# A fused kernel's third block: attention in six batches, with the input blocks reordered between them

## The chip, the cores and the metric

One Trainium2 chip, one core. The metric is the device time of the whole program in microseconds (us), the median of three runs. The program is one launch that computes three transformer blocks one after the other on 256 tokens of width 1024.

## What is computed

The first two blocks (a pooling mixer with a SwiGLU, and latent attention with a SwiGLU) and what follows the third block's mixer (cross-attention to a memory of 256 tokens, an FFN with a convolution, the last norm) are not touched. The third block's mixer is, cut to what matters:

```python
z = rms_norm(x, mix_norm_g) @ w_in                      # 256 x 1024 by 1024 x 2328
q, kc, vc, ks, vs, kw, vw, gl, zg, zc = split(z)        # 512, 6 x 128, 24, 512, 512

# attention: 8 heads of 64, two groups of 4 heads share keys and values
k_cmp, v_cmp = compress(kc), compress(vc)               # 15 blocks of 32 tokens, gelu MLP
o_c = softmax(mask(q @ k_cmp)) @ v_cmp
o_s = softmax(causal(q @ ks)) @ vs                      # all 4 blocks of 64 are selected
o_w = softmax(causal(q @ kw)) @ vw                      # the window is longer than the sequence
y_nsa = g[..., 0] * o_c + g[..., 1] * o_s + g[..., 2] * o_w     # g = sigmoid(gl)

# gMLP: u, v = gelu(zg); per chunk of 128 tokens and group: a causal 128 x 128 matrix
y_gmlp = u * (w_s @ layer_norm(v) + b_s)

# convolution: a, gt = zc; 31 taps along the tokens, each of 256 channels by itself
y_conv = silu(layer_norm(conv31(a * sigmoid(gt))))

y = concat(rms_norm(y_nsa), rms_norm(y_gmlp), rms_norm(y_conv))
x = x + y @ w_out
```

Everything is float32.

## The kernel before, in words

**Engines and order.** Each engine has its own program, written out by hand: SP issues the weight loads, ACT, DVE, POOL (GpSimd) and PE follow, and semaphores tie them. An engine runs its instructions in the written order, so what waits holds up all that is written behind it.

**Weights** come as blocks of 1 MB (`raw`, three buffers). ACT rounds a block to its upper part `wh` (L555), DVE subtracts to get the lower part `wl` (L968). A call `after(name)` in ACT's or DVE's program makes the part of the block three places behind `name`. PE multiplies a block as three products, upper by upper, upper by lower, lower by upper (`three`, L1629 to L1631): 48 matmuls of 256 columns for a block, 24 for the narrow z_gl. Blocks of the mixer are z_a and z_gt (the convolution's two inputs), z_v and z_u (the gMLP's), z_kcvc (to be compressed), z_q0 and z_q1 (queries), z_ksw and z_vsw (keys and values of both branches), z_gl (gates); then mem6 and mem7, the last two blocks of the memory's values, and four of `w_out`.

**The convolution** is shared. `hc` = a * sigmoid(gt) (two channel halves, c = 0 and 1) is made by DVE at L1264 from z_gt's tanh on ACT (L785). DVE does all 31 taps of c = 0. POOL does the taps 0 to 24 of c = 1, a multiplication (L1581) and an addition (L1584) for each, and DVE the last six of c = 1 (L1282). DVE's list is `VECTOR_TAPS`: 25 taps of c = 0, then in turn (25,0), (25,1), (26,0), ... Tap (25,1) waits for POOL's last one. Fourteen of DVE's 37 taps are written ahead of the attention loop, then four in each unit, so (25,1) comes in unit 3.

**The attention** is a loop of 16 units, one for each head and branch. In a unit DVE adds the mask to the scores in the bank and takes the row maxima in one custom instruction (L1383), negates (L1386); ACT exponentiates (L849) and sums; DVE makes the reciprocal times the gate (L1392, L1393); ACT scales the probabilities by it (L863); PE transposes them (3 of 128x128, L2087); ACT copies them to SBUF (L857); PE multiplies by the values (3 products, L2099 to L2101) into the two banks in which the compressed branch already lies. Scores run two units ahead (L2048). Between transposes and P.V stand nine matmuls of mem6 or mem7, or four dummy matmuls of 512 columns (`turn_over`, L2120), 24 in all.

**The rest of the mixer.** The compressed branch: four transfers of kc and vc on ACT's queue, 64 small matmul records (L2004), scores (L2026), softmax on DVE (L1360 ff.), eight transfers on ACT's queue that place v_cmp as a block diagonal `vbd` (L830), and the product with it (L2079). The gMLP: gelu of z_v and z_u (DVE L1290 to L1295), the mix (L2064, L2068). The output product reads `yn`, turned on PE (L1646) and split in upper and lower parts (ACT L575, DVE L977).

The list, and how a tap waits:

```python
VECTOR_TAPS = ([(k, 0) for k in range(POOL_TAPS)]
               + [(k, c) for k in range(POOL_TAPS, TAPS) for c in range(2)])
                        if (k - 1, c) in VECTOR_TAPS:
                            dve.wait_ge(cv_tap, VECTOR_TAPS.index((k - 1, c)) + 1)
                        else:
                            dve.wait_ge(cv_tap_pool, k)
```

Of the kernel before, what the change touches and what calls it, by code (L numbers as in the profile page):

```python
# [75 lines left out]
TAPS_BEFORE = 14  # L76
TAPS_PER_STEP = 4
# [4 lines left out]
U_MEM = {6: 3, 7: 9}  # L82
MEM_PER_STEP = 3
MEM_STEPS = -(-NT * KD // MEM_PER_STEP)

U_TURN, U_STATS, U_LN, U_SILU, U_SQUARES, U_TURN_Y, U_SPLIT = 7, 8, 9, 10, 11, 13, 14
# [56 lines left out]
def weight_blocks(w):  # L143
# [59 lines left out]
    cols("z_v", win, zg + GW, GW)  # L203
    cols("z_u", win, zg, GW)
    cols("z_kcvc", win, z, 2 * P)
# [4 lines left out]
    cols("z_gl", win, z + 6 * P, 24)  # L210
    mem(6)
# [11 lines left out]
def build(nc, w, consts, bands, out):  # L223
# [17 lines left out]
    with ExitStack() as ctx:  # L241
# [17 lines left out]
        ksw = sb("ksw", [P, GROUPS, 2, SEQ])  # L259
        con = sb("con", [P, NCONST])  # L260
# [12 lines left out]
        REGION = 61312  # L273
# [4 lines left out]
        def at_(name, shape, dt=F32, off=None):  # L278
# [4 lines left out]
            for d in shape[1:]:  # L283
# [56 lines left out]
        kcm = at_("kcm", [P, NCMP])  # L340
# [6 lines left out]
        p2_0 = at_("p2_0", [P, 3 * P])  # L347
# [7 lines left out]
        s2 = [kvc[:, :, :].rearrange("p a s -> p (a s)")[:, 0:3 * P],  # L355
              fl[:, :, :, :, :].rearrange("p a k g n -> p (a k g n)")[:, GG * P:GG * P + 3 * P]]
        p2 = [p2_0, at_("p2_1", [P, 3 * P])]
        nst = at_("nst", [P, 4, 2 * NSA_HEADS, NT])
        lst = at_("lst", [P, 64])

        uu, vg = yn[:, :, 3 * GW:4 * GW], yn[:, :, 0:GW]
        ws = fl[:, :, :, :, :].rearrange("p a k g n -> p (a k g n)")[:, 0:GG * P]
# [171 lines left out]
        def _(act):  # L534
# [248 lines left out]

            act.wait_ge(block_used, at["z_gt"] + 1)
            act.activation(e1[:, :], bank[1][:, :], ACT.Tanh, scale=0.5).then_inc(z_out, 1)  # L785
            hi(at["z_a"] + 3)
            after("z_gt")
            for i, name in enumerate(("z_v", "z_u")):
                act.wait_ge(block_used, at[name] + 1)
                b = bank[2 + i]  # L790

                act.wait_ge(*((hc_done, 1) if i == 0 else (gz_d, 3)))
                act.activation(e1[:, :], b[:, :], ACT.Square).then_inc(gz_a, 1)
                act.wait_ge(gz_d, 3 * i + 2)
                act.activation(e1[:, :], e2[:, :], ACT.Tanh, scale=GELU_S).then_inc(gz_a, 1)
                after(name)
            act.wait_ge(block_used, at["z_kcvc"] + 1)
            act.activation(kvc[:, :, :].rearrange("p a s -> p (a s)"), bank[0][:, :], ACT.Copy).then_inc(z_out, 1)
            act.wait_ge(z_out, 2)
            for g in range(GROUPS):  # L800

                act.dma_start(x4[0:DH, :, g, :], kvc[g * DH:(g + 1) * DH, :, :]).then_inc(shifted, 16)
                act.dma_start(x4[DH:P, :, g, 0:SEQ - 1], kvc[g * DH:(g + 1) * DH, :, 1:SEQ]).then_inc(shifted, 16)
            after("z_kcvc")
            for i in range(2):
                act.wait_ge(block_used, at[f"z_q{i}"] + 1)
                act.activation(qt[:, 2 * i:2 * i + 2, :].rearrange("p a s -> p (a s)"), bank[1 + i][:, :],
                               ACT.Copy).then_inc(z_out, 1)
                after(f"z_q{i}")

            act.wait_ge(cmp_mm, 1)
            hs = bank[7][0:DH, 0:60]
# [3 lines left out]
            act.wait_ge(block_used, at["z_ksw"] + 1)  # L816
            act.wait_ge(ksw_zero, 1)
            for g in range(GROUPS):
                rows_ = slice(g * DH, (g + 1) * DH)
                ins = act.activation(ksw[rows_, g, :, :].rearrange("p a s -> p (a s)"), bank[3][rows_, :], ACT.Copy)  # L820
            ins.then_inc(z_out, 1)
            after("z_ksw")
            act.wait_ge(cmp_mm, 2)
# [129 lines left out]
        def _(dve):  # L953
# [1302 lines left out]
```

## Time and profile before

| | |
|---|---|
| median of 3 runs | 968.39 us (966.55, 968.39, 970.23) |
| the profiled execution | 968.99 us, of which the profile's span is 967.0 us |
| mean granted clock of PE over the span | 0.989 |
| PE busy in the span | 917.7 us |
| the mixer's stretch on PE | 540.16 (first matmul of z_a) to 699.37 us |

Times in the rows are us from the span's start. A row's duration of a matmul is longer than the distance to the next one's start, since matmuls overlap, so distances between starts are what they cost. "x3" is a count of records; a float32 product outside `three` is recorded as more than one.

### The profile page before, as it was taken

The page shows a single profiled execution, that of the slowest core. Times are in us where ns is not written, and L with a number is a line of the kernel's source. Part 1 is how long each engine was busy: PE and PEld are TensorE (multiplying, and loading weights), DVE is VectorE, ACT ScalarE, POOL GpSimd, SP SyncE. Part 2 cuts the span into 40 slices and gives each one's busy share as a digit, 9 for nine tenths or more (in the row PEclk, how much of TensorE's full clock was granted, in tenths as well). Part 3 has the DMA queues.
Part 4 walks back from the last instruction along what each step waited for, and adds up shares of the span by engine and source line. Part 5 has one row for each costly group of instructions (what it writes and reads, how often), then busy time and mean ns, then how long its engine had stood idle before and what let it go on. Part 6 is the DMA issues. An engine that isn't in the chain of part 4 may idle for free. (4 is left out here: it accounts for less than half of the span.)

```text
span 967.0 us, 16772 instructions
## 1 busy us (share of the span) xinstructions
PE 917.7 (95%) x6406; PEld 852.4 (88%) x6406; DVE 536.5 (55%) x882; ACT 476.7 (49%) x768; POOL 339.5 (35%) x189
## 2 busy tenths in 40 slices
PE   4999999999999999999999999897999989999996
PEld 4999999999987899999999999686798789999995
DVE  3884443345556574444435495775465576666655
ACT  5754444334555574334444442586454465555542
POOL 2264333440000064444333279701100154444441
PEclk9999999999999999999999999798999999999999
DMA  9677665642431767666644665201343577666601
GB/s 305 201 230 227 195 193 179 182 130 81 148 131 45 226 202 233 179 184 195 194 154 131 176 157 187 88 1 44 131 174 87 153 215 214 179 178 192 195 23 43
DMA packets 187405, 154.33 MB, mean 160 GB/s; under 512 B 6573, under 2 KB 172685, under 8 KB 187357
## 3 DMA queue, kind: packets, MB, share of 16 engines
q1 hardware_dynamic: 184941, 148.67, 50.6%
q0 software_dynamic: 752, 2.39, 1.0%
q10 hardware_dynamic: 1664, 2.60, 0.8%
q8 instruction: 33, 0.54, 0.3%
q14 instruction: 15, 0.12, 0.0%
HBM read 152.04 MB, written 1.05 MB: 158 GB/s over the span
## 5 line engine op out<-in xcount | busy, mean ns | idle before, releaser
L1538 POOL TENSOR_TENSOR dl<-draw,dh 128x1024 fp32r<-128x1024 f32 x66 | 241.4, 3659 | 287.0 <-ACT dh L599 286.9
L1629 PE MATMUL bank<-xh,wh 128*128 128x256 f32 x1192 | 338.1, 284 | 1.4 <-DVE xl L1189 0.7
L1631 PE MATMUL bank<-xh,wl 128*128 128x256 f32 x1192 | 337.1, 283 | 0.0
L1630 PE MATMUL bank<-xl,wh 128*128 128x256 f32 x1192 | 337.0, 283 | 0.0
L1629 PEld LDWEIGHTS bank<-xh,wh 128*128 128x128 f32 x1192 | 227.4, 191 | 4.8 <-DVE wl L968 1.3
L1630 PEld LDWEIGHTS bank<-xl,wh 128*128 128x128 f32 x1192 | 227.6, 191 | 2.2
L1631 PEld LDWEIGHTS bank<-xh,wl 128*128 128x128 f32 x1192 | 227.6, 191 | 0.1
L968 DVE TENSOR_TENSOR wl<-raw,wh 128x2048 fp32r<-128x2048 f32 (+5 forms) x53 | 112.4, 2127 | 60.4 <-ACT wh L555 60.4
L1068 DVE TENSOR_TENSOR wl<-raw,wh 128x2048 fp32r<-128x2048 f32 x57 | 137.5, 2412 | 1.4 <-ACT wh L622 1.4
L622 ACT ACTIVATE wh<-raw 128x2048 fp32r<-128x2048 f32 x57 | 108.8, 1909 | 8.5 <-DMA raw<-in_ffn_w_up 8.5
L1629 PE MATMUL bank<-dh,hh 128*128 128x512 f32 x264 | 103.4, 392 | 3.7 <-DVE hl L1074 3.7
L1631 PE MATMUL bank<-dh,hl 128*128 128x512 f32 x264 | 103.4, 392 | 0.0
L1630 PE MATMUL bank<-dl,hh 128*128 128x512 f32 x264 | 103.3, 391 | 0.0
L555 ACT ACTIVATE wh<-raw 128x2048 fp32r<-128x2048 f32 (+5 forms) x53 | 93.6, 1772 | 19.2 <-PE bank L1631 8.3
L608 ACT ACTIVATE th<-bank 128x256 f32<-128x256 f32 x44 | 16.8, 382 | 173.9 <-PE bank L1631 171.7
L1518 POOL TENSOR_SCALAR st<-ss 128x1 f32<-128x1 f32 x18 | 10.8, 602 | 236.2 <-ACT junk L564 236.1
L1058 DVE SCALAR_TENSOR_TENSOR ga<-th,bank 128x256 f32<-128x256 f32 x44 | 18.5, 420 | 134.9 <-ACT th L608 134.9
L599 ACT ACTIVATE dh<-draw 128x1024 fp32r<-128x1024 f32 x66 | 69.6, 1055 | 10.7 <-PE bank L1631 10.7
L1074 DVE TENSOR_TENSOR hl<-pr,hh 128x256 fp32r<-128x256 f32 x66 | 29.8, 452 | 63.5 <-ACT hh L636 63.5
L1629 PEld LDWEIGHTS bank<-dh,hh 128*128 128x128 f32 x264 | 49.8, 189 | 12.9 <-issue 4.0
L1629 PE MATMUL bank<-wh,xh 128*128 128x512 f32 (+3 forms) x182 | 60.0, 330 | 0.0
L1631 PEld LDWEIGHTS bank<-dh,hl 128*128 128x128 f32 x264 | 49.6, 188 | 10.8
(301 smaller groups left out, 1440.3 us busy)
## 6 DMA issues: line engine op xcount, KB each, us to landing
raw<-in_ffn_w_up SPq DMA_DIRECT2D x88, 512.0 KB, 6.1
draw<-in_ffn_w_down SPq DMA_DIRECT2D x66, 512.0 KB, 3.5
raw<-in_ffn_w_gate SPq DMA_DIRECT2D x44, 512.0 KB, 5.3
raw<-in_w_in SPq DMA_DIRECT2D x18, 512.0 KB, 5.0
raw<-in_xattn_wk SPq DMA_DIRECT2D x8, 512.0 KB, 4.7
raw<-in_mla_w_o SPq DMA_DIRECT2D x8, 512.0 KB, 3.9
raw<-in_xattn_wv SPq DMA_DIRECT2D x8, 512.0 KB, 4.5
raw<-in_w_out SPq DMA_DIRECT2D x8, 512.0 KB, 4.4
```

Source lines behind the costliest of these rows:

```text
L555: ins = act.activation(h, r, ACT.Copy)
L599: act.activation(dh[s][:, :], draw[s][:, :], ACT.Copy).then_inc(d_hi, 1)
L608: act.activation(th[s][:, :], b[:, 0:SEQ], ACT.Tanh, scale=0.5).then_inc(tanh_done, 1)
L622: act.activation(wh[ns][:, :], raw[ns][:, :], ACT.Copy).then_inc(hi_done, 1)
L968: ins = dve.tensor_tensor(l, r, h.bitcast(F32), ALU.subtract)
L1058: dve.scalar_tensor_tensor(out=ga[:, :], in0=th[s][:, :], scalar=1.0, in1=g, op0=ALU.add, op1=ALU.mult).then_inc(gated, 1)
L1068: dve.tensor_tensor(wl[ns][:, :], raw[ns][:, :], wh[ns][:, :].bitcast(F32), ALU.subtract).then_inc(lo_done, 1)
L1074: dve.tensor_tensor(hl[s][:, :], pr[s][:, :], hh[s][:, :].bitcast(F32), ALU.subtract) \
L1538: pool.tensor_tensor(dl[s][:, :], draw[s][:, :], dh[s][:, :].bitcast(F32), ALU.subtract) \
L1629: pe.matmul(outp, a_hi, b_hi, start=start, stop=False, **kw)
L1630: pe.matmul(outp, a_hi, b_lo, start=False, stop=False, **kw)
L1631: return pe.matmul(outp, a_lo, b_hi, start=False, stop=stop, **kw)
```

## The change

The mixer is written in another order, and its attention in another form.

- The blocks' order becomes z_a, z_gt, z_q0, z_q1, z_ksw, z_vsw, z_gl, z_kcvc, z_v, z_u, mem6, mem7. z_vsw, z_v, z_u, mem6 and mem7 are multiplied in two halves, with pieces of attention between them.
- The attention goes in six batches (`BATCHES`: token tile t, branch, first head, heads in each group). A batch has two banks, one for each group, each with 512 columns of scores: four heads by 128 keys (t = 0) or two by 256 (t = 1). PE starts a bank with identity times mask (`identr`, `maskr`) and adds the scores. DVE takes the maxima with one reduction for a bank, ACT exponentiates straight from the bank, PE turns four tiles, ACT copies 512 columns, PE multiplies by the values. Reciprocal and gate are applied behind P.V (`acc_evict`), the compressed branch is added by DVE (`comp_add`).
- The dummy matmuls, the scaling of the probabilities and the custom maxima are gone.
- DVE's taps are placed by `conv(first, last)` between the blocks' parts. POOL does its 25 taps in one piece; the load and cut of w_s stand ahead of them, the load of the last norm's gain behind the attention.
- The eight `vbd` transfers stand on ACT behind the exponentials of batch 3.

The diff, cut (a line of "..." marks what is left out):

```diff
+BATCHES = ((0, 0, 0, 4), (0, 1, 0, 4), (1, 0, 0, 2), (1, 0, 2, 2), (1, 1, 0, 2), (1, 1, 2, 2))
+HEADS_DONE = [sum(GROUPS * x[3] for x in BATCHES[:b]) for b in range(len(BATCHES) + 1)]
...
@@ ACT's program @@
+            def nsa_exp(b, g):
+                t, br, j0, n = BATCHES[b]
...
+                for j in range(n):
+                    h = g * REP + j0 + j
+                    act.activation(s2[g][:, j * keys:(j + 1) * keys], bank[g][:, j * keys:(j + 1) * keys], ACT.Exp,
+                                   scale=NSA_SCALE, bias=nst[:, 1, t, br, h:h + 1],
+                                   accum_out=nst[:, 2, t, br, h:h + 1]).then_inc(n_exp, 1)
...
+            nsa_pt(2, 1)
+            gelu_tanh(1)
+            nsa_exp(3, 1)
+            after("z_u")
             act.wait_ge(cmp_mm, 2)
...
             for h in range(NSA_HEADS):
                 act.dma_start(vbd[h * NCMP:(h + 1) * NCMP, h * DH:(h + 1) * DH], vcs[:, h // REP, :]) \
                    .then_inc(vbd_set, 16)
...
+            nsa_pt(3, 0)
+            nsa_exp(4, 0)
...
@@ DVE's program @@
+            def acc_evict(t, br):
+
+                dve.wait_ge(o_all, (2, 4, 8, 12)[2 * t + br])
+                r = nst[:, 3, t, br, :]
+                then(dve.reciprocal(r, nst[:, 2, t, br, :]))
+                then(dve.tensor_tensor(r, r, gv[:, t, 1 + br, :], ALU.mult))
...
+                if br == 1:
+                    dve.wait_ge(acc_out, 2 * t + 2)
+                    return dve.tensor_tensor(yn[:, t, 0:HALF], yn[:, t, 0:HALF], acc2[:, :], ALU.add)
...
+            conv(24, 26)
+            after("z_gl")
+            nsa_max(1)
...
             after("z_kcvc")
+            conv(26, 29)
+
+            gelu_in(0)
+            nsa_max(2)
+            gelu_out(0)
...
+            after("mem7")
+            dve.wait_ge(comp_in, NT)
+            acc_evict(1, 1).then_inc(y_nsa, 1)
+            split_t(6, xh, xl, C_MOUT, 0, range(4, KD))
...
@@ POOL's program @@
             pool.wait_ge(hc_done, 1)
-            conv(0, 2)
+            conv(0, POOL_TAPS)
             layer_norm_rstd(0, 12, 20)
-            conv(2, 11)
...
@@ PE's program @@
+            def nsa_scores(b):
+                t, br, j0, n = BATCHES[b]
+                keys = (t + 1) * P
+                pe.wait_ge(n_exp, HEADS_DONE[b])
+                for g in range(GROUPS):
+
+                    o = bank[g][:, :].rearrange("p (j s) -> p j s", j=n)[:, :, t * P:keys]
+                    pe.matmul(o, identr[:, :], maskr[:, :].rearrange("p (a s) -> p a s", a=1).to_broadcast([P, n, P]),
+                              start=True, stop=False, skip_group_check=True)
+                    for j in range(n):
+                        ins = pe.matmul(bank[g][:, j * keys:(j + 1) * keys], qt[:, j0 + j, t * P:(t + 1) * P],
+                                        ksw[:, g, br, 0:keys], start=False, stop=True, skip_group_check=True)
+                ins.then_inc(n_mm, 1)
...
+            nsa_turn(1, 1)
+            nsa_pv(1, 0)
+            pe.wait_ge(gz_d, 3)
+            tokens_half("z_u", 3, 0, xh, xl)
+            nsa_pv(1, 1)
+
+            nsa_scores(3)
+            nsa_turn(2, 0)
+            tokens_half("z_u", 3, 1, xh, xl)
...
+            pe.wait_ge(y_scaled, 4)
+            turn(yn, 0, range(4, KD))
```

How the instructions stand now, at three places. DVE, from the weight pass behind z_kcvc to gelu_out of z_v (`yc` is the convolution's sum, `e_...` are the gelu's scratch tiles, `x_111` holds the gMLP's u and v, `nst` the maxima):

```order
L988 TENSOR_TENSOR wl<-raw,wh 128x2048 [waits hi_done,fl_done]
L1302 SCALAR_TENSOR_TENSOR yc<-hc,col,yc 128x256 [waits cv_tap_pool]
L1302 SCALAR_TENSOR_TENSOR yc<-hc,col,yc 128x256 [waits cv_tap] x2
L1319 TENSOR_SCALAR e_127<-e_125 128x512 [waits gz_a]
L1321 TENSOR_TENSOR e_126<-e_127,bank 128x512 [waits gz_d]
L1311 TENSOR_REDUCE nst<-bank 128x2 [waits n_mm]
L1311 TENSOR_REDUCE nst<-bank 128x2
L1315 TENSOR_SCALAR nst<-nst 128x2x2 [waits dve_order]
L1325 SCALAR_TENSOR_TENSOR x_111<-e_125,bank 128x512 [waits gz_a]
```

Before, the tap that waits for POOL stood in the attention loop, in unit 3, between the maxima of one unit and the reciprocals (DVE, before):

```order
L1386 TENSOR_SCALAR nst<-nst 128x2 [waits dve_order]
L1282 SCALAR_TENSOR_TENSOR yc<-hc,col,yc 128x256 [waits cv_tap_pool]
L1282 SCALAR_TENSOR_TENSOR yc<-hc,col,yc 128x256 [waits cv_tap] x3
L1392 RECIPROCAL nst<-nst 128x2 [waits n_exp]
L1393 TENSOR_TENSOR nst<-nst,gate 128x2 [waits dve_order]
```

The tap moved to a place ahead of gelu_in, of the maxima of batch 2 and of gelu_out. PE, from the scores of batch 2 to z_u's first half (`s_0`, `s_1` are the exponentials of the two groups, `gain` the room of the copied probabilities, `con` the identity):

```order
L2046 MATMUL bank<-maskr,identr 128x2x128 [waits n_exp]
L2049 MATMUL bank<-ksw,qt 128x256 x2
L2046 MATMUL bank<-maskr,identr 128x2x128
L2049 MATMUL bank<-ksw,qt 128x256 x2
L2059 MATMUL bank<-con,s_0 128x128 [waits n_out,n_exp]
L2059 MATMUL bank<-con,s_0 128x128 x3
L2123 MATMUL bank<-fl,cw_113 64x30 [waits z_ws,fl_done]
L2123 MATMUL bank<-fl,cw_113 64x30 x31
L2059 MATMUL bank<-con,s_1 128x128 [waits n_out,n_exp]
L2059 MATMUL bank<-con,s_1 128x128 x3
L2072 MATMUL bank<-vsw,gain 128x64 [waits n_out]
L2072 MATMUL bank<-vsw,gain 128x64 x3
L1662 MATMUL bank<-wh,xh 128x256 [waits lo_done,gz_d]
```

The semaphore `gz_d` is counted by the gelu's steps on DVE; z_u's first matmul waits for L1325 above. ACT, around the `vbd` transfers, before:

```order
L824 ACTIVATE kcm<-bank 128x15 [waits cmp_mm]
L825 ACTIVATE vcs<-bank 15x128
L830 DMA vbd<-vcs 15x64 [waits vbd_zero,cmp_out]
L830 DMA vbd<-vcs 15x64 x7
L833 ACTIVATE vsw<-bank 128x512 [waits block_used]
```

and now:

```order
L879 ACTIVATE vcs<-bank 15x128
L883 DMA vbd<-vcs 15x64 [waits cmp_out]
L883 DMA vbd<-vcs 15x64 x7
L820 ACTIVATE gain<-bank 128x512 [waits o_all,n_t]
L812 ACTIVATE s_0,nst<-bank,nst 128x256 [waits n_t,n_max]
L812 ACTIVATE s_0,nst<-bank,nst 128x256
```

What stands behind the transfers is now the copy of batch 3's probabilities and batch 4's exponentials; before, it was the copy of z_vsw.

## Rows read from the trace of the kernel before

**Rows 1.** page, part 1: busy time, share of the span, instructions
```profile
PE 917.7 (95%) x6406; PEld 852.4 (88%) x6406; DVE 536.5 (55%) x882; ACT 476.7 (49%) x768; POOL 339.5 (35%) x189
```

**Rows 2.** windows: stretch, length, busy us (records) of each engine, clock, DMA, GB/s
```profile
540.16:604.00 63.84, 62.93 (x563) 61.75 (x562) 40.91 (x52) 23.24 (x28) 39.71 (x36) 1.00 0.64 183
...
608.80:619.00 10.20, 9.49 (x25) 5.44 (x24) 6.09 (x20) 2.72 (x11) 9.39 (x10) 0.51 0.56 205
619.00:663.40 44.40, 37.95 (x279) 35.18 (x280) 31.05 (x126) 32.14 (x100) 7.22 (x11) 1.00 0.07 25
663.40:666.80 3.40, 3.40 (x17) 3.22 (x17) 2.06 (x11) 2.12 (x8) 0.39 (x1) 0.54 0.02 5
...
677.00:699.37 22.37, 21.10 (x98) 17.19 (x96) 11.06 (x14) 10.01 (x14) 2.17 (x5) 1.00 0.43 142
```

**Rows 3.** waits of PE, 540 to 702: total us, times, longest
```profile
PE bank L2099 <- ACT p L857: 7.6, 5, 2.6
```

**Rows 4.** timeline of PE: start, us, line, operation, count
```profile
563.20 0.28 PE L1629 MATMUL bank<-xh,wh 128*128 128x256 f32 x1
...
580.57 3.92 PE L2004 MATMUL bank<-fl,cw 128*64 128x30 f32 x64
...
632.56 0.50 PE L2087 MATMUL bank<-con,kvc 128*128 128x128 f32 x3
632.90 0.82 PE L2048 MATMUL bank<-ksw,qt 128*128 128x128 f32 x4
633.37 0.47 PE L1629 MATMUL bank<-wh,mh 128*128 128x256 f32 x1
...
635.23 0.50 PE L2087 MATMUL bank<-con,fl 128*128 128x128 f32 x3
...
682.03 0.40 PE L1631 MATMUL bank<-wh,xl 128*128 128x512 f32 x1
682.26 0.40 PE L1629 MATMUL bank<-wh,xh 128*128 128x512 f32 x1
```

**Rows 5.** groups of PE by form, 540 to 700: busy, mean ns, idle before
```profile
L2004 PE MATMUL bank<-fl,cw 128*64 128x30 f32 x64 | 3.9, 221 | 0.0
L2079 PE MATMUL bank<-vbd,e 120*128 120x512 f32 x4 | 3.8, 1101 | 0.5 <-ACT e L844 0.5
L2026 PE MATMUL bank<-kcm,qt 64*128 64x15 f32 x32 | 3.3, 259 | 0.0
```

**Rows 6.** timeline of ACT: z_gt's tanh, and the vbd transfers' issue
```profile
551.88 0.60 ACT L785 ACTIVATE e<-bank 128x512 f32<-128x512 f32 x1 [9.12 <-PE bank L1631]
...
593.98 8.88 ACTq L830 DMA_DIRECT2D vbd<-vcs  x8
```

**Rows 7.** timeline of DVE: product hc, a weight pass, taps
```profile
558.72 0.68 DVE L1264 SCALAR_TENSOR_TENSOR hc<-e,bank 128x512 f32<-128x512 f32 x1
...
605.34 2.41 DVE L968 TENSOR_TENSOR wl<-raw,wh 128x2048 fp32r<-128x2048 f32 x1 [3.66 <-ACT wh L555]
...
621.36 2.65 DVE L1282 SCALAR_TENSOR_TENSOR yc<-hc,col,yc 128x256 f32<-128x256 f32 x4
...
631.83 1.67 DVE L1282 SCALAR_TENSOR_TENSOR yc<-hc,col,yc 128x256 f32<-128x256 f32 x4
```

**Rows 8.** groups of POOL by form, 553 to 626
```profile
L1581 POOL TENSOR_SCALAR tapped<-hc,col 128x256 f32<-128x256 f32 x24 | 33.0, 1376 | 2.1
L1584 POOL TENSOR_TENSOR yc<-yc,tapped 128x256 f32<-128x256 f32 x24 | 21.5, 894 | 2.0
```

**Rows 9.** timeline of POOL in its taps
```profile
605.70 3.10 POOL L1581 TENSOR_SCALAR tapped<-hc,col 128x256 f32<-128x256 f32 x1
...
615.74 0.92 POOL L1581 TENSOR_SCALAR tapped<-hc,col 128x256 f32<-128x256 f32 x1
...
617.57 0.92 POOL L1581 TENSOR_SCALAR tapped<-hc,col 128x256 f32<-128x256 f32 x1
...
622.26 0.86 POOL L1584 TENSOR_TENSOR yc<-yc,tapped 128x256 f32<-128x256 f32 x1
```

More of the change, by code:

```diff
@@ new lines, in _ @@
+            nsa_exp(1, 0)
+            after("z_kcvc")
+            nsa_pt(0, 1)
+            nsa_exp(1, 1)
+            gelu_square(0)
+            nsa_pt(1, 0)
+            gelu_tanh(0)
+            nsa_exp(2, 0)
+            after("z_v")
+            nsa_pt(1, 1)
+            nsa_exp(2, 1)
+            act.wait_ge(cmp_mm, 1)
+            hs = bank[2][0:DH, 0:60]
+            act.activation(hg[:, 0, :], hs, ACT.Square).then_inc(cmp_a, 1)
+            act.wait_ge(cmp_d, 2)
+            act.activation(hg[:, 1, :], hg[:, 2, :], ACT.Tanh, scale=GELU_S).then_inc(cmp_a, 1)
@@ L895, in _ @@
-            act.wait_ge(o_all, 2 * NSA_HEADS)
+            nsa_pt(3, 1)
+            nsa_exp(4, 1)
+            nsa_pt(4, 0)
+            mem_block(6)
+            after("mem6")
+            nsa_exp(5, 0)
+            nsa_pt(4, 1)
+            nsa_exp(5, 1)
+            act.wait_ge(pc_t, NT)
+            act.activation(pct[0:120, :], bank[2][0:120, 0:SEQ], ACT.Copy).then_inc(pc_out, 1)
+            act.wait_ge(cvln_done, 1)
+            act.activation(e1[:, :], e2[:, :], ACT.Tanh, scale=0.5).then_inc(cv_a, 1)
@@ L1251, in _ @@
             times_gain()
+            dve.memset(kcm[:, :, :], 0.0)
             dve.memset(vbd[:, :], 0.0).then_inc(vbd_zero, 1)
@@ new lines, in comp_add @@
+            def comp_add(t):
+                dve.wait_ge(o_cmp, t + 1)
+                return dve.tensor_tensor(yn[:, t, 0:HALF], bank[2 + t][:, :], yn[:, t, 0:HALF], ALU.add)
+            conv(0, 2)
+            after("z_gt")
+            conv(2, 8)
+            after("z_q0")
+            conv(8, 12)
+            after("z_q1")
+            conv(12, 18)
+            after("z_ksw")
+            nsa_max(0)
+            conv(18, 24)
+            after("z_vsw")
+            conv(24, 26)
+            after("z_gl")
@@ L1307, in _ @@
+            nsa_max(3)
             dve.wait_ge(ln_rs, 1)
@@ new lines, in _ @@
+            pe.wait_ge(t_lo, KD * 6)
+            columns("z_a", 4, xh, xl)
+            columns("z_gt", 5, xh, xl)
+            columns("z_q0", 2, xh, xl)
+            columns("z_q1", 3, xh, xl)
+            pe.wait_ge(ws_cut, 1)
+            for g in range(GG):
+                ins = pe.transpose(bank[0][:, g * P:(g + 1) * P], ws[:, g * P:(g + 1) * P], ident)
+            ins.then_inc(ws_t, 1)
+            columns("z_ksw", 6, xh, xl)
+            pe.wait_ge(mem_out, 6)
+            tokens_half("z_vsw", 7, 0, xh, xl)
@@ L2148, in _ @@
+                pe.matmul(bank[2 + t][:, :], pct[0:120, t * P:(t + 1) * P], vbd[0:120, :], start=True, stop=True) \
+                  .then_inc(o_cmp, 1)
+            nsa_pv(5, 1)
+            pe.wait_ge(comp_in, NT)
+            pe.wait_ge(y_scaled, 4)
+            turn(yn, 0, range(4, KD))
             pe.wait_ge(t_lo, KD * 6 + 4)
```

632 lines of the change are left out of this document (291 added, 341 removed).

## The prediction

> **What bounds the kernel now.** I read the page first. TensorE (PE) is busy 917.7 us, 95% of the span [rows 1], so time is won only where PE idles, does work that can go, or runs at the lower clock. The windows of the third block's mixer come next [rows 2]: from 540.16 to 604 PE is busy 62.93 of 63.84 us at full clock; from 608.8 to 619 it shows a granted clock of 0.51 (that is 1.2 of 2.4 GHz) while it issues small matmuls; a later stretch of 3.4 us is at 0.54; the output projection fills the rest. The waits say what most of the pauses were [rows 3]: 7.6 us for the transposed probabilities before P.V (L2099), the longest 2.6. The chain that ended last is PE's as well, so I sum along PE from 540.16 to 699.37 (the first transpose of norm 5, where the last window of [rows 2] ends), and add waits where another engine must be late.
>
> **Prices.** [Rows 4] Three weight blocks of 48 matmuls take 580.57 - 563.20 = 17.37 us, 5.79 each or 0.12 a matmul, 2.9 for a half; z_gl, 24 matmuls of the same length, 2.9. One attention unit with nine memory matmuls takes 635.23 - 632.56 = 2.67; nine at 0.12 are 1.08; 1.59 is left for 3 transposes, 2 score products, 3 P.V products. Output matmuls of 512 columns start 0.23 apart, 96 are 22.1, and the 24 filler matmuls of the same width 5.5. [Rows 5] The compressed branch's 64 records cost 3.9, its scores 3.3; both stay. A mask product isn't in the trace. It is a matmul of 512 or 256 columns, so 0.23 or 0.12; not below 0, since an instruction comes on, and not above the 0.4 that a record of 512 columns lasts. I take the pitch: four of 0.23 and eight of 0.12, 1.9 in all.
>
> **What the change removes.** The filler (5.5), most of the waits for probabilities (7.6) [rows 3], ACT's 32 scalings and four of its 16 copies of probabilities, DVE's custom maxima and per-unit reciprocals. DVE gets 2 reductions for a batch, ACT 32 exponentials from the banks. DVE and ACT have room: in the first window they are busy 40.91 and 23.24 of 63.84 [rows 2], so I price these at nothing, covered by PE's blocks. If that cover went, they would cost a unit's wait of up to 2.6 again [rows 3].
>
> **What the change makes wait.** The convolution's channel half c=1 is done by POOL for 25 taps, and DVE goes on with tap (25,1). DVE's program now has that tap before gelu_in(0), nsa_max(2) and gelu_out(0), and PE's z_u waits for gelu_out(0). Behind it on DVE stand all further maxima, on PE all later products. So POOL's last tap is on the path.
>
> *When POOL is done.* Its start moves forward: z_gt's tanh begins at 551.88 and lasts 0.60 [rows 6], and the product hc is now the next thing on DVE (before, two weight passes stood ahead, and it came at 558.72 [rows 7]); with its 0.68 hc stands at 553.2. POOL's 25 taps are 33.0 us for the multiplication and 21.5 for the addition [rows 8], the first tap's single 0.7, and some 0.08 between the 49 records, 59.0. Their length isn't their own. Undisturbed, taps start 617.57 - 615.74 = 1.83 apart, 45.8 for 25 [rows 9]; but the multiplication at 605.70 took 3.10 while DVE's weight pass of 2.41 ran from 605.34 [rows 7, 9]. Beside DVE's own taps POOL's addition took 0.86 where the undisturbed pitch leaves 1.83 - 0.92 - 0.2 = 0.71, and those four DVE taps took 2.65, 0.66 each, where four without POOL took 1.67 [rows 7, 9]. After the change six weight passes of 2.3 fall into POOL's taps, seven before, so the length is bounded by 45.8 and about 60. I take 59.0, since the nearest rows are the same instructions beside the same passes: done at 612.3.
>
> *DVE after that.* Three taps at 0.4 (1.2), then two steps of gelu_in, two maxima over 512 columns of a bank, and gelu_out. Each of the five is taken at hc's 0.68 [rows 7] (3.4). z_u may start at 616.9.
>
> *When PE gets there.* 540.16 + eight blocks 46.3 + z_gl 2.9 + ws and gate transposes 0.7 + masks 1.2 + compressed branch 3.9. Of the attention, a third of the transposes, half of the score columns and a quarter of P.V stand ahead; in a unit they are 0.34, 0.47 and the remaining 0.78 long by their starts [rows 4], so 16 x (0.11 + 0.24 + 0.20) = 8.7. And one short hold for the gates: they stand on DVE behind nsa_max(1), 2 x 0.68 + 0.4 less PE's transposes of 0.4, 1.4. Sum 605.3. **The hold is 616.9 - 605.3 = 11.6 us**: it eats nearly all that filler and waits gave.
>
> *After it.* Attention 25.4 - 8.7 = 16.7, masks 0.7, z_u 5.8, mem6 and mem7 11.6, compressed second layer 0.7, its scores 3.3, mix about 2.9 at full clock, small transposes 0.6, the product with vbd (3.78 at half clock [rows 5]) 1.9, yn's transposes 1.8, output 22.1: 68.1. Holds:
> - The eight vbd transfers are issued by ACT; before, ACT's queue was in them 8.88 us [rows 6], and nothing of PE's waited for what stood behind. Now nsa_pt(3,0) stands behind them, and PE's turn(3,1) and P.V(3,0) wait for it. PE has the scores of batch 4, turn(3,0) and 16 score products (3.3) to do in that time, so about 5.0 is open. Its bounds are 0 (if the issues run ahead of PE) and 8.9.
> - The last two copies of probabilities, behind mem7's copy and split: 2.0, by the longest waits of [rows 3], up to 2.6.
> - acc_evict(1,1) (three steps, the two large ones 0.7 each) and the transposed halves' split on DVE now stand before the output product: 3.5, between 1.4 (the two large steps alone) and 5.8 (DVE still in mem7's pass of 2.3).
> - Norm 5: 1.3.
>
> 11.8 in all: 616.9 + 68.1 + 11.8 = 696.8. The clock: behind one of the waits for probabilities PE ran 3.4 us at 0.54 [rows 2], 1.6 lost. The three long holds should each do that: 4.8. The stretch at 0.51 is then not counted (that is a rival). End 701.6 against 699.37, **+2.2**. The later part of the program is the same in both; the final gain's transfer moves behind the attention on POOL's queue, and is used only by the last norm, at the program's end: nothing. 968.99 for the profiled execution + 2.2 = **971.2 us**; that execution lies 0.6 over the median 968.39 of the three, so nothing is corrected.
>
> **A rule against the change.** The row shows: POOL's multiplication 3.10 where 0.92 is undisturbed, and 0.15 more on the addition beside DVE's taps [rows 9]. The Trainium skill, "SBUF — State Buffer", section Who interferes with whom, says that a DVE instruction with two inputs in SBUF contends with a GpSimd instruction that reads SBUF, and that whichever issued first keeps the other out for its whole length. By that rule each of DVE's 25 own taps would hold POOL for its full time too; the trace bears this out for the weight passes, and only in part for the taps. It is rival 3.
>
> **Rivals.**
> 1. *No hold, faster.* POOL's taps go undisturbed, because they start earlier and the passes fall between them: 25 x 1.83 = 45.8, done at 599.0, DVE's chain at 603.6, before PE's 605.3. Then 11.6 and one 1.6 for the clock are gone: 971.2 - 13.2 = **958.0**. For it: 1.83 is what [rows 9] show whenever DVE makes no pass. Against it: DVE's six passes must run in that very time, as PE's blocks need them. Half ways (POOL done at 605) give a value between. Chance 0.21.
> 2. *Slower, by the clock.* After the holds PE has mostly small products: compressed scores 3.3, mix 2.9, transposes and P.V about 1.2 between them, and no filler any more. Before, mix, transposes and the vbd product stood at 0.51 for 10.2 us [rows 2]. If the 7.4 us of it run at 1.2 GHz they take 14.8; less the 1.6 already counted, +5.8: **977.0**. It decides as soon as the hold for vbd is there and PE comes out of it slow: then the small products don't bring the clock back until mem6's second half. The Trainium skill, "TensorE: Matmul & The Clock Gate", Part 1, calls the slow state the default, which activity lifts; this trace agrees in that 0.51 stood over the small matmuls and 1.00 came back after the vbd products. Chance 0.29.
> 3. *The port.* If DVE's taps block POOL fully, POOL needs 45.8 + 6 x 2.3 + 25 x 0.41 = 69.9, done at 623.1, 10.8 later: 971.2 + 10.8 = **982.0**. Against it: by the same count before, seven passes and some twenty taps, 70, it took 59. Chance 0.03.
> 4. *The change doesn't do what it says*: the DVE tap's wait isn't met at its place, or several of the holds I sum fall into each other. Remainder 0.03, spread to both sides.
>
> **How the numbers follow.** Forecast 971.2 with 0.44. No change is within 0.5% (4.8 us of 968.39, about what a measurement of this kernel can tell), so 963.5 to 973.2. The forecast's own spread: POOL's end 3 either way, vbd's hold 0 to 8.9; mostly 965 to 975, of which what passes 973.2 is set off against what of rival 2 stays below. Faster: rival 1 and a little of the remainder, 0.22. Slower: rivals 2 and 3 with the rest, 0.34. Same 0.44. Range 960 to 979: it leaves out the full rival 1 (about 0.12, its half ways stay in), rival 3 and the far part of rival 2 (0.08).
>
> **What will show it.** In the profile after: DVE's convolution line with a wait of some 15 us for POOL's tap; POOL's last tap at about 612; PE's waits with one of about 11 us before the tokens product of z_u, released by DVE's gelu_out; one of about 5 us before a probabilities transpose, with ACT in issues behind it; about 3.5 before the output product. The windows after 617 show whether the clock is at 0.5 over the scores and the mix (rival 2) or 1.0. Wrong: no wait before z_u (rival 1), or POOL later than 618 (rival 3), or PE waiting for maxima in the middle batches, which I priced at nothing.

## The result, and the profile after

| | before | changed |
|---|---|---|
| median of 4 runs | 969.01 us (966.55 to 970.23) | 978.0 us (976.05 to 978.36) |
| span of the profiled execution | 967.0 us | 974.2 us |
| its granted clock of PE, mean | 0.989 | 0.981 |

The ratio is 1.01, with a 95% interval from 1.0079 to 1.012: the change makes the kernel 9 us slower. The forecast was 971.2, its range 960 to 979; rival 2 had stood at 977.0. The profiled execution of the changed kernel took 976.05, the fastest of its four; the other three have a mean clock of 0.975 to 0.977.

PE's row of the page after answers to [rows 1]:

```profile
PE 914.4 (94%) x6394; PEld 852.0 (87%) x6394; DVE 534.9 (55%) x805; ACT 463.5 (48%) x735; POOL 334.9 (34%) x189
```

PE's busy time fell by 3.3 us while the span grew by 7.2, so the loss is idle time, and part of the busy time is at the lower clock. The waits of PE from 530 to 720, the mixer and the first transposes behind it, for [rows 3] (the line, what ended the wait, us in total, times, the longest):

```profile
PE bank L1662 <- DVE x L1325: 9.0, 1, 9.0
PE bank L2059 <- ACT gain L820: 3.8, 1, 3.8
PE bank L1662 <- DVE xl L997: 3.7, 1, 3.7
PE bank L1679 <- DVE xn L1007: 2.9, 3, 1.3
PE bank L2072 <- ACT gain L820: 1.7, 1, 1.7
PE bank L1662 <- DVE gate L1366: 1.6, 1, 1.6
```

Five short waits for copied probabilities (7.6 us in all) have become one long wait for gelu_out(0) (L1325), one behind the vbd transfers (L2059), one before the output product (L997), and two short ones. The windows of the same stretch (stretch, length, busy us of each engine, granted clock, DMA share, GB/s), for [rows 2]:

```profile
540.45:596.00 55.55, 53.90 (x449) 52.99 (x448) 39.79 (x47) 27.00 (x54) 39.90 (x36) 1.00 0.64 180
596.00:616.40 20.40, 11.35 (x120) 10.74 (x119) 8.65 (x13) 3.48 (x13) 14.39 (x15) 0.81 0.15 52
616.40:620.00 3.60, 3.60 (x21) 3.60 (x21) 3.30 (x9) 3.38 (x9) 0.93 (x2) 0.63 0.00 0
620.00:640.00 20.00, 18.41 (x149) 17.52 (x147) 16.05 (x34) 6.81 (x17) 0.00 (x0) 0.99 0.30 106
640.00:657.00 17.00, 14.80 (x55) 12.47 (x56) 3.05 (x10) 3.31 (x11) 0.00 (x0) 0.51 0.01 3
657.00:675.65 18.65, 16.98 (x136) 15.44 (x134) 12.78 (x24) 11.69 (x27) 2.12 (x4) 1.00 0.17 57
675.65:679.40 3.75, 0.04 (x2) 0.04 (x1) 3.65 (x10) 2.73 (x8) 1.41 (x4) 1.00 0.56 178
679.40:705.20 25.80, 24.55 (x104) 19.89 (x105) 10.36 (x14) 9.98 (x14) 1.54 (x4) 0.93 0.35 117
```

From 640 to 657 the clock stands at 0.51, for 17 us, of which PE is busy 14.8; before, such a stretch was 10.2 us long. That is the largest piece that the main sum had left out. The chain that ended last, by engine, for the whole span; by line it leads through POOL's taps (L1622 3%, L1625 2%) and ACT's transfers (L883, 1%):

```profile
PE 77%; POOL 7%; DVE 7%; ACT 4%; issue 3%; DMA 1%; ACTq 1%; SPq 0%; DVEq 0%
```

The chain of the kernel before is followed only from about 659 us on, so the two chains can't be compared over the attention.

Now the path to the long wait, as the timelines of POOL, DVE and PE have it (start, length, line):

```profile
553.66 0.67 POOL L1618 TENSOR_SCALAR yc<-hc,col 128x256 f32<-128x256 f32 x1 [5.20 <-DVEq L1287]
...
561.83 2.84 POOL L1622 TENSOR_SCALAR tapped<-hc,col 128x256 f32<-128x256 f32 x1
...
610.94 0.72 POOL L1625 TENSOR_TENSOR yc<-yc,tapped 128x256 f32<-128x256 f32 x1
```

```profile
611.70 1.27 DVE L1302 SCALAR_TENSOR_TENSOR yc<-hc,col,yc 128x256 f32<-128x256 f32 x3 [11.61 <-POOL yc L1625]
...
615.34 0.68 DVE L1325 SCALAR_TENSOR_TENSOR x<-e,bank 128x512 f32<-128x512 f32 x1
```

```profile
616.08 0.58 PE L1662 MATMUL bank<-wh,xh 128*128 128x256 f32 x1 [9.05 <-DVE x L1325]
```

POOL's 25 taps took from 553.66 to 611.66, 58.0 us; DVE stood 11.6 us at tap (25,1), came to gelu_out 3.6 us later, and PE began z_u at 616.08, 9.05 us after it had finished the first group's P.V of batch 1.

And the second hold, ACT and then PE:

```profile
634.04 7.31 ACTq L883 DMA_DIRECT2D vbd<-vcs  x8
641.46 0.60 ACT L820 ACTIVATE gain<-bank 128x512 f32<-128x512 f32 x1 [7.44 <-issue]
```

```profile
634.76 3.64 PE L2154 MATMUL bank<-kcm,qt 128*128 128x15 f32 x32
642.20 1.09 PE L2059 MATMUL bank<-con,s 128*128 128x128 f32 x4 [3.79 <-ACT gain L820]
643.08 1.81 PE L2072 MATMUL bank<-vsw,gain 128*128 128x64 f32 x8
```

ACT is in the eight issues for 7.31 us; the copy of batch 3's probabilities comes behind them, and PE waits 3.79 us for it. Four transposes last 0.60 at full clock; here they last 1.09.

### The profile page after: what moved, and what is told of

Read it like the earlier page. It is cut to its first block, busy times and chain, and to the rows that moved or that the text cites. A ratio compares the mean times of both kernels' runs of the same rounds, so it can differ in the third digit from the quotient of the medians.

```text
span 974.2 us, 16639 instructions
## 1 busy us (share of the span) xinstructions
PE 914.4 (94%) x6394; PEld 852.0 (87%) x6394; DVE 534.9 (55%) x805; ACT 463.5 (48%) x735; POOL 334.9 (34%) x189
## 4 chain that ended last, share of the span: by engine, by line
PE 77%; POOL 7%; DVE 7%; ACT 4%; issue 3%; DMA 1%; ACTq 1%; SPq 0%; DVEq 0%
PE bank L1662 23%; PE bank L1664 23%; PE bank L1663 23%; POOL tapped L1622 3%; POOL yc L1625 2%; DMA raw<-in_pool_w 1%; PE bank L1754 1%; DVE wl L988 1%; PE bank L1679 1%; DVE xl L997 1%; ACTq L883 1%; PE bank L2252 1%; POOL st L1555 1%; PE bank L2072 1%; ACT wh L554 1%
## 5 line engine op out<-in xcount | busy, mean ns | idle before, releaser
L598 ACT ACTIVATE dh<-draw 128x1024 fp32r<-128x1024 f32 x66 | 69.7, 1056 | 10.6 <-PE bank L1664 10.6
L1662 PEld LDWEIGHTS bank<-dh,hh 128*128 128x128 f32 x264 | 49.8, 189 | 12.9 <-issue 4.0
L1664 PE MATMUL bank<-wh,xl 128*128 128x512 f32 (+3 forms) x182 | 59.7, 328 | 0.0
```

Of the source, the lines that this page charges most:

```text
L598: act.activation(dh[s][:, :], draw[s][:, :], ACT.Copy).then_inc(d_hi, 1)
L1662: pe.matmul(outp, a_hi, b_hi, start=start, stop=False, **kw)
L1664: return pe.matmul(outp, a_lo, b_hi, start=False, stop=stop, **kw)
```

## The experiments

Each run is told with its own median and that of the kernel before in the same series of runs (before: 970.0 for a1 to a4, 968.37 for b1 to b4, 969.37 for c1 to c4), and the difference of the two. The change itself stands at 978.0 - 969.01 = +9.0; what an edit is worth is the distance from there, by these differences. A trace shows one execution of a kernel.

### a1: the last taps later

```diff
             after("z_kcvc")
-            conv(26, 29)
-
             gelu_in(0)
...
             after("z_v")
-            conv(29, 33)
...
             after("z_u")
-            conv(33, len(VECTOR_TAPS))
+            conv(26, len(VECTOR_TAPS))
```

> Only DVE's eleven last convolution taps move: all stand behind the weight pass that follows z_u, so that neither gelu_in(0), the maxima nor gelu_out(0) wait for POOL's tap 24. Theory (POOL's last tap is on the path by way of gz_d): PE's 9.0 us before z_u are gone, PE starts z_u at about 607, and the stretch behind it runs at full clock, 1.6 more; the time falls from 978 by about 10.6 to 967. Rival (the wait only hides another one, for the maxima, the exponentials or the weight pass behind it): PE waits at z_u or within the next 10 us for something else, and less than 4 us are won. The wait of about 3.8 before the transposes of batch 3 and the clock of 0.5 behind it stay in either case.

Measured: 966.15 against 970.0, -3.9, ratio 0.9971 (0.9956 to 0.9985). The edit is worth 12.9 us, more than the 10.6 expected; 1.0 of it lies in the two medians of the kernel before. PE's waits in its trace:

```profile
PE bank L2056 <- ACT gain L820: 4.3, 1, 4.3
PE bank L1659 <- DVE xl L997: 3.7, 1, 3.7
```

PE's first matmul of z_u, without a wait:

```profile
606.74 0.36 PE L1659 MATMUL bank<-wh,xh 128*128 128x256 f32 x1
```

The wait before z_u is gone, and z_u begins at 606.74 although POOL's last tap ends even later than in the change, at 613.89. That POOL's last tap held PE, through DVE's order and gz_d, is shown: only the place of DVE's taps changed. The rival falls; no new wait stands in its place. The wait behind vbd and the slow stretch behind it stay (4.3 us; from 628.8 to 645.9 at 0.50).

### a2: the vbd transfers later

```diff
             nsa_pt(3, 1)
             nsa_exp(4, 1)
+            act.wait_ge(cmp_out, 2)
+            for h in range(NSA_HEADS):
+                act.dma_start(vbd[h * NCMP:(h + 1) * NCMP, h * DH:(h + 1) * DH], vcs[:, h // REP, :]) \
+                   .then_inc(vbd_set, 16)
```

(and the same lines taken away ahead of nsa_pt(3, 0).)

> Only the eight vbd transfers move on ACT: from ahead of the copy of batch 3's probabilities to behind the exponentials of batch 4, where ACT had 12 us without work. The 9.0 us before z_u stay. The wait of 3.8 before L2059 goes in any case. Theory A (the clock falls because PE stood still for those 3.8 us): the small products from 640 to 657 run at 1.00 instead of 0.51, 7 us more are won, in all 11: about 967. Theory B (the clock falls because the small products, scores with 15 columns and the mix with 64, keep PE too little at work by themselves): only the 3.8 us go, 974, and the windows still show about 0.5 over the mix.

Measured: 971.55 against 970.0, +1.6, ratio 1.0041 (1.0021 to 1.006). The edit is worth 7.4 us, between the two theories. Its nine runs lie in two groups, five at 971.2 to 971.6 and four at 975.1 to 976.0; by their mean, 973.2, it would be 5.8. The profiled execution is one of the five. The wait of 3.8 is gone. The windows from the 15-column products on:

```profile
634.90:639.60 4.70, 4.70 (x46) 4.70 (x44) 4.60 (x11) 1.20 (x4) 0.00 (x0) 1.00 0.55 180
639.60:649.90 10.30, 10.30 (x38) 8.41 (x37) 3.19 (x10) 2.21 (x8) 0.00 (x0) 0.50 0.08 25
649.90:668.00 18.10, 16.43 (x129) 14.97 (x127) 11.31 (x24) 11.50 (x26) 2.12 (x4) 1.00 0.18 59
```

PE is busy for the whole of the first two windows, 4.70 of 4.70 and 10.30 of 10.30, and the clock is still at 0.50 in the second. So theory A, that the clock fell for the pause, doesn't hold as it was put. In the change the clock fell at about 639.5, here at 639.6, both 4.8 us after the 15-column products began, with the pause and without. So the pause didn't start the slow stretch. Without it the stretch is 10.3 us instead of 17, and of the 6.7 between them 2.2 are the pause itself.

### a3: both

> Both edits: taps late, vbd transfers later. If the two costs lie one after the other on PE's path, the gains add: 978 less 10.6 less 11 (theory A of the clock) is 956, or 978 less 10.6 less 3.8 is 963.5 (theory B). If one covers the other (DVE's eleven taps, now in one piece behind z_u, hold up the maxima of batch 4), a new wait of 2 to 4 us shows before the transposes of batch 4.

Measured: 961.6 against 970.0, -8.4, ratio 0.9928 (0.9901 to 0.9954). The two edits alone gave 12.9 and 7.4, together 17.4 of 20.3, so they nearly add; no new wait came. The windows:

```profile
600.00:624.93 24.93, 24.93 (x227) 23.67 (x227) 16.99 (x34) 12.35 (x30) 14.20 (x15) 1.00 0.25 85
624.93:630.00 5.07, 5.07 (x47) 5.00 (x46) 5.07 (x10) 0.60 (x1) 0.00 (x0) 1.00 0.48 170
630.00:640.80 10.80, 10.80 (x39) 8.81 (x40) 6.02 (x18) 2.82 (x10) 0.00 (x0) 0.53 0.07 22
```

This is the cleanest view of the fall: PE is busy without a break from 600 to 640.8, the 15-column products begin at 624.93 and last 3.6 us, four transposes and P.V of 64 columns follow, and from 630.0 the clock is at half. In the slow window stand the mix, P.V and the scores of batch 5.

### a4: split before the last eviction

```diff
+            split_t(6, xh, xl, C_MOUT, 0, range(4, KD))
             acc_evict(1, 1).then_inc(y_nsa, 1)
-            split_t(6, xh, xl, C_MOUT, 0, range(4, KD))
```

> As the run with both edits, and at the end DVE splits the transposed gMLP and convolution halves before it takes the last part of the attention from its bank (acc_evict(1,1)), instead of behind it. Theory: the 3.7 us before the output product are acc_evict's 1.8 and the split's; with the split first, 1.8 are won, and the attention part, 1.7 later, is still hidden behind the first two output blocks (11 us). Rival: it isn't hidden, and the transposes of the attention part wait instead; nothing is won.

Measured: 960.16 against 970.0, -9.8, ratio 0.9906 (0.988 to 0.9932). Against a3 1.4 us, which is near the 1.8 expected but inside what such medians scatter. The trace shows the step itself: the wait before the output product fell from 3.7 to 2.5, so 1.2, not 1.8. The rival falls: the transposes of the attention part show no wait. The slow stretch behind the 15-column products is longer here than in a3, 13.5 us (627.9 to 641.4, PE busy throughout), with nothing changed up to there.

### b1: wide products among the small ones

```diff
             ins.then_inc(sc_mm, 1)
+            tokens_half("mem6", 7, 1, mh, ml)
             nsa_turn(3, 1)
...
             nsa_turn(4, 0)
-            tokens_half("mem6", 7, 1, mh, ml)
```

> On top of a4 (taps late, vbd later, split first) one piece of PE's work moves: the second half of mem6 (24 matmuls of 256 columns, 2.9 us) stands between the 15-column score products and the transposes of batch 3, instead of behind the mix. No work is added. In a3 and a2 the clock fell to 0.5 about 5 us after the 15-column products began, with PE never idle, and stayed there for 10 us. Theory (the run of small products takes the clock down): broken by the wide products, it stays at 1.00 or falls for a shorter stretch, up to 5 us are won: 955 to 957. Rival 1 (the 15-column products do it by themselves): the fall comes at about the same distance behind them, and lasts as long: 960. Rival 2: the piece is missed where it stood, PE waits for the copy of batch 4's probabilities, and a part is given back.

Measured: 957.6 against 968.37, -10.8, ratio 0.9909 (0.9873 to 0.9945). Its windows:

```profile
621.00:627.70 6.70, 6.69 (x52) 6.30 (x52) 4.61 (x8) 3.16 (x7) 0.00 (x0) 1.00 0.18 53
627.70:631.20 3.50, 3.50 (x19) 3.50 (x18) 3.46 (x10) 0.00 (x0) 0.00 (x0) 0.51 0.50 198
631.20:662.00 30.80, 25.45 (x181) 22.06 (x181) 20.93 (x46) 17.07 (x44) 4.91 (x6) 1.00 0.22 70
```

The clock still falls behind the 15-column products, but is back after 3.5 us, and the mix and the scores behind it run at 1.00. In a4's profile the lower clock stood for 13.5. So with wide products in between the stretch is ten us shorter in the trace. Of the time only about 1 us more than a4 is seen (-10.8 against -9.8), less than the intervals, and 957.6 lies between the theory's 955 to 957 and rival 1's 960: the time doesn't decide between them. The profiled execution was the fastest of four, and the slower ones had a lower mean clock of PE: 956.02 us at 0.992, 961.38 at 0.987. So in some executions the clock is lower for longer, and the trace above is that of a good one. Rival 2 is there too, in small: two waits for the copy of probabilities, 1.0 in all.

### b2: dummy matmuls before the mix

```diff
             pe.wait_ge(gz_d, 6)
+            for _ in range(8):
+                pe.matmul(bank[3][:, :], mh[:, 0, 0:P], mh[:, 0:2, :], start=True, stop=True, skip_group_check=True)
```

> On top of a4 eight dummy matmuls of 512 columns (their result isn't used) stand before the mix, at full clock 1.9 us of work that computes nothing. Theory (the kernel before kept its clock by such filler): the clock stays at 1.00 through the mix and the scores of batch 5, 5 us come back for 1.9 spent: 957. Rival (what fell is set by the 15-column products, which lie ahead of the filler): the clock falls all the same, the filler itself runs at the lower clock and costs up to 3.8: 962 to 964.

Measured: 959.08 against 968.37, -9.3, ratio 0.9919 (0.9892 to 0.9947), and its nine runs lie widely. They go by the mean clock: 953.96 us at 0.997, 957.43 at 0.992 (the profiled one, with one short fall as in b1), 963.93 at 0.986. With the filler the clock stays up in some executions and not in others, and by its median it isn't told apart from a4. This stays inconclusive.

### b3: gates first, last copy first

```diff
@@ DVE @@
-            nsa_max(1)
             dve.wait_ge(gl_t, 1)
             dve.tensor_scalar(gate[:, :, :], ...
+            nsa_max(1)
@@ ACT @@
+            nsa_pt(5, 1)
             mem_block(7)
             after("mem7")
-            nsa_pt(5, 1)
```

> On top of a4 two places in the order: DVE makes the gates before the maxima of batch 1 instead of behind them, and ACT copies the last probabilities (nsa_pt(5,1)) before mem7's copy and the rounding behind it. Each should take away the wait that it stood for: 1.65 us before z_v, 1.7 before the last P.V: 3.3 in all, 957. Rival: the 1.65 before z_v are given back, since PE then waits for the transfers of kc and vc or POOL's tap is not earlier, and only 1.7 stay: 958.5.

Measured: 961.81 against 968.37, -6.6, ratio 0.9933 (0.9911 to 0.9954): 3.2 us worse than a4, not 3.3 better. Both waits are gone, and two others stand in their place:

```profile
PE bank L1659 <- DVE xl L997: 2.6, 1, 2.6
PE bank L2043 <- ACT s L812: 2.1, 1, 2.1
PE bank L1676 <- DVE xn L1007: 2.1, 2, 1.3
PE bank L1676 <- DVE yn L1479: 1.1, 1, 1.1
```

The 2.1 before a mask product is a wait for the exponentials of an earlier batch: I take it that PE came 1.65 earlier, and ACT and DVE didn't. The granted clock:

```profile
621.20:648.40 27.20, 26.38 (x99) 23.20 (x100) 12.82 (x29) 6.50 (x19) 0.00 (x0) 0.50 0.11 41
```

The wait of 2.1 ended at 622.02; behind it come the scores of batch 4 and, from 626.88, the 15-column products, and the clock was down for 27 us. My expectation had no such thing. In this execution a pause of 2 us ahead of a run of small products went with a loss of many times its length. It was the slowest of six, 964.54 against the median 961.81, so 27 us is the long end; the median is 3.2 worse than a4's.

### b4: all edits, vbd on POOL

```diff
@@ POOL @@
             layer_norm_rstd(0, 12, 20)
+            pool.wait_ge(cmp_out, 2)
+            for h in range(NSA_HEADS):
+                pool.dma_start(vbd[h * NCMP:(h + 1) * NCMP, h * DH:(h + 1) * DH], vcs[:, h // REP, :]) \
+                    .then_inc(vbd_set, 16)
             layer_norm_rstd(1, 40, 44)
```

(with a1, a4, b1 and b3's edits.)

> All edits together, and the eight vbd transfers are issued by POOL behind the first layer norm's factor instead of by ACT. If each gain is its own: 960 less 3.3 less up to 5 is 952 to 957. If POOL's issues hold up its layer norm, a wait of some us appears at DVE's e<-bank (L1466) and before the vbd product.

Measured: 957.79 against 968.37, -10.6, ratio 0.991 (0.9879 to 0.9941). The wait of 2.2 before the mask product is here too (until 622.21), but with the wide products among the small ones the slow stretches behind it are about 6 and 3 us, where b3 had 27. POOL is in the eight issues for 4.12 us, where ACT took 7.31. No wait for POOL shows among PE's, and of the waits that I had feared on DVE there is one of 0.9 us. As a whole it is no better than b1, and 0.8 above the 952 to 957 expected.

### c1 and c2: the copy alone, the scores in two halves

c1 is b1 with ACT's part of b3 alone. c2 is c1 with mem6's half between the two groups' 15-column products:

```diff
                     ins = pe.matmul(bank[2][:, c:c + NCMP], qt[:, j, t * P:(t + 1) * P], kcm[:, g, :], start=True, stop=True)
+                if g == 0:
+                    tokens_half("mem6", 7, 1, mh, ml)
             ins.then_inc(sc_mm, 1)
-            tokens_half("mem6", 7, 1, mh, ml)
```

> On top of b1 (957.6) ACT copies the last probabilities before mem7's copy and rounding; the gates stay where they were. In b3 both were moved and a new wait of 2.1 before the masks of batch 3 came, with the clock down from 621. Theory: that wait came from the gates' edit (PE earlier, the exponentials not), and the copy by itself wins its 1.9: 955.7. Rival: the 1.9 comes back one step later, as the 1.1 before the attention part's transposes that b3 showed: 956.8 or more.

> On top of c1 the sixteen 15-column products are in two halves of eight, with mem6's second half between them. Theory (a long enough run of them takes the clock down): the last fall behind them, 627.5 to 631.5 in b1, is gone too, 1.7 won: 954. Rival (it came from the few us before them, with the masks and scores of batch 4): it stays, 955.7.

Measured: c1 958.23 against 969.37, -11.1, ratio 0.9887 (0.9849 to 0.9926); c2 957.43, -11.9, ratio 0.989 (0.9847 to 0.9933). c1 has no 2.1 before the masks (0.2 is left), so that wait in b3 was the gates' doing, as supposed; but the 1.9 won at the last copy comes back as 1.1 before the attention part's transposes, as its rival had it. For c2 the windows are:

```profile
618.00:657.50 39.50, 34.71 (x269) 31.61 (x267) 28.13 (x58) 20.29 (x51) 2.12 (x4) 1.00 0.17 55
657.50:664.50 7.00, 5.84 (x14) 4.61 (x15) 3.65 (x9) 1.27 (x4) 2.14 (x5) 0.51 0.54 192
```

In its profiled execution the clock stays at 1.00 over the 15-column products, the mix, the scores of batch 5 and a new wait of 2.3 for a copy of probabilities (639.0 to 641.3). It falls only at 657.5, in the wait of 2.6 before the output product, for 7 us. That isn't shown to be the split's doing. In c1's profiled execution, where the sixteen 15-column products stand in one piece, the clock doesn't fall behind them either; it is at 1.00 from 618 to 636.8 and then at 0.50 for 3.2 us, over the scores of batch 5. And b1, with PE's order the same as c1's, fell at 627.7. So where the clock falls differs between executions of nearly the same program. c2's median lies above both that were expected, 954 and 955.7, and b1, c1 and c2 can't be told apart by their times.

### c3: the wide products moved in the change itself

The same move as in b1, made in the changed kernel with nothing else.

> The change as it was, with only mem6's second half moved to stand behind the 15-column products. It fills 2.9 of the 3.8 us in which PE waited for ACT behind the vbd transfers. Theory (small products with the wait together took the clock down from 640 to 657, 8.5 us lost): the wait is 0.9, the loss falls to 2 to 5 us: 978 less 2.9 less 3.5 to 6.5 is 968.5 to 971.5. Rival (the clock falls the same with wide products ahead, by the 9.0 us hold at z_u and the mix alone): only 2.9, 975.

Measured: 971.21 against 969.37, +1.8, ratio 1.0025 (1.0008 to 1.0043): 7.2 us better than the change, by the place of 24 matmuls. The wait behind vbd is 0.9 where it was 3.8 (both waits for L820 before transposes together), so 2.9 of the 7.2 are the pause filled. Some 4 are left, which I put down to the clock. The profiled execution, 1.4 slower than the median, shows this only in part: behind the 15-column products the clock is at half for 3.2 and 6.7 us, where the change had 14.3 of busy time, but it is at half for another 9.6 around the wait before the output product, where the change had 3.3. The 9 us before z_u are untouched (9.2).

### c4: the kernel before without its filler

```diff
-                if spare:
-                    turn_over()
```

(both places.)

> The kernel before with its 24 dummy matmuls left out, nothing else: what one part of the change is worth alone. The prediction priced them at 5.5 us of PE's path. Theory 1 (they are plain work on the path): 969 less 5.5 is 963.5. Theory 2 (they fill waits for the copy of the probabilities, and keep the clock): the waits grow by what they covered and the granted clock falls in the units from 619 to 633 and 655 to 667; the time stays within 2 us of 969 or rises.

Measured: 969.59 against 969.37, ratio 1.001 (0.9992 to 1.0028). Leaving out 24 matmuls that compute nothing wins nothing. Two of its waits, and the window in which it now runs slowly:

```profile
PE bank L2099 <- ACT p L857: 9.5, 7, 2.6
...
PE bank L2087 <- ACT kvc L863: 1.9, 2, 1.5
```

```profile
626.30:633.10 6.80, 6.33 (x28) 5.96 (x29) 6.40 (x26) 4.36 (x14) 0.00 (x0) 0.52 0.01 4
```

Against [rows 3] the waits for copies grew by 1.9 us, those before transposes by 1.3 (0.6 before), and 6.8 us at 0.52, which were at 1.00 before, cost half their length, 3.3. A wait before the mix (L2064) shrank from 1.5 to 0.6. Together 5.6, which takes back the 5.5 of the filler. So theory 2 holds.

## Why the prediction was right or wrong

The time, 978.0, lay in the range, 1.0 from its upper end, but not near the forecast of 971.2: the range had been drawn to take in rival 2. Of the directions "same", which I thought likeliest (0.44), didn't come, but "slower" (0.34). By its steps:

- **POOL's end.** Predicted 612.3, measured 611.66; hc at 553.2, POOL's first tap began at 553.66. 59.0 for 25 taps, measured 58.0. Right. Beside a weight pass a POOL instruction took 2.84, where [rows 9] had 3.10.
- **The hold before z_u.** Predicted z_u at 616.9 and PE's arrival at 605.3, measured 616.08 and 607.03; 11.6 became 9.05. The mechanism was right, and a1 shows it by an experiment. PE's arrival was put 1.7 early.
- **The hold behind vbd.** Predicted 5.0, measured 3.79; eight issues took 7.31 us, where before they took 8.88. Right in place, and a2 shows it: with the transfers elsewhere the wait is gone.
- **The end.** 2.0 before the last P.V, measured 1.67; 3.5 before the output product, measured 3.71.
- **The clock: the term that was too small.** "The three long holds should each do that: 4.8. The stretch at 0.51 is then not counted (that is a rival)." Two of the three did about that: from 616.08 to 619.5, behind the hold at z_u, 1.5 was lost, and from 680.3 to 683.6, in the output product, 1.7. The middle one didn't: from 642.20 to 656.5 PE was busy for 14.3 us at 0.50, and lost 7.2. Together 10.4, or 5.6 more than the 4.8. It was lost over transposes, the mix, P.V and scores. That is rival 2, priced at +5.8. I held it for less likely than the forecast (0.29 against 0.44), although [rows 2] showed the mix and the vbd product at 0.51 for 10.2 us; a row that shows an effect on the same instructions should have carried the main sum. The reason that I gave for it, that PE comes out of the hold slow, isn't what the runs show: in a2 and a3 the clock falls with PE busy throughout, and in a2 as long after the 15-column products' start as in the change.
- **The work behind z_u.** From 616.08 to norm 5's transposes at 705.22 are 89.1 us. Less the waits (3.79, 1.67, 3.71, 1.27: 10.4) and less those 10.4 of the clock it is 68.3, where I had 68.1.
- **The sum.** The mixer ended at 705.22, 3.6 after my 701.6: z_u began 0.8 earlier, the waits behind it were 1.4 shorter, the work 0.2 longer, the clock cost 5.6 more. So two misses of mine in the other direction hid 2.2 of it.
- **What the change removes.** I said the filler and the waits gave about 13 us that the hold "eats". The sum itself was made along PE and didn't use that, but as a reading it was wrong for the filler: c4 shows that in the kernel before it was worth nothing.
- **Rival 1** (POOL undisturbed, 45.8) fell: the taps took 58.0. **Rival 3** (each of DVE's taps holds POOL fully, 623.1) fell too: POOL was done at 611.66. **Whatever I priced at nothing** in DVE and ACT was covered: no wait for maxima shows among PE's waits.
- **Outside the mixer.** The stretch's end is 5.8 us later than before, the span 7.2. In the profiled execution PE has one more slow stretch, at 772.7 to 776.2, busy 3.50 of 3.50 at 0.52, 1.7 us lost; my sum had nothing there. Why it falls there I haven't tested. With the 3.6 of the mixer this makes the profiled execution 976.05, 4.9 above the forecast of 971.2. The median is another 2 above that, and its executions have the lower mean clocks; no trace of them is there to say where.

## What to carry to other kernels

When work moves between engines' orders, follow every wait on a slow helper's last step through to what stands behind it on the waiting engine: here one tap, moved up in DVE's program, cost 13 us (a1), and its cure was three lines. Price a run of small matmuls at the clock that the trace shows for such a run, not at the clock of its neighbours. Putting wide products that are needed anyway among them gave 7.2 us by itself (c3), a part of it by filling a wait; a pause at their front was seen to cost much in one profile (b3). The best of these versions have the taps late, the vbd transfers later, the split first and mem6's half among the small products (b1, 957.6), with the last copy first as well in c2 (957.4). They take about 1% less than the kernel before, and 2% less than the change.

## What the runs showed of the hardware that I had not expected

- PE's clock falls to half without any pause: in a3 PE is busy 24.93 of 24.93 us, then 5.07 of 5.07 over products of 15 columns, four transposes and P.V of 64 columns, and then at 0.53 while still busy 10.80 of 10.80. The Trainium skill, "TensorE: Matmul & The Clock Gate", Part 1, describes the clock by idle and active; this trace differs, and it decides here: what went before the fall was a run of instructions with few columns, without a break between them.
- With a wait of 2.1 us ahead of such a run the slow stretch was 27 us long in b3 and about 6 in b4, with one of 3.8 in its middle 17 (the change), with none 10 to 14 (a2, a3, a4), and with wide products in between 3.5 (b1) or 3.2 and 6.7 (c3). In c1 and c2 the clock didn't fall behind the 15-column products at all, and in c2 a wait of 2.3 left it at 1.00. These are single profiled executions.
- Executions of one kernel differ by how long the clock is down. b2: 953.96 us at a mean clock of 0.997, 963.93 at 0.986. a2: 971.2 to 971.6 at 0.984 or 0.981, 975.1 to 976.0 at 0.977 to 0.979. Gains of 1 or 2 us between such kernels aren't settled here.
